# Cross attention's first scores inside the last query set, and masked attention's weight copies ahead of its scalings

## The reference, cut to what matters

```python
# masked ("sparse") attention: 8 heads of 64, one key/value head, blocks of 128 queries;
# each query sees its top keys by an index score
logits = q @ k_sel * 64 ** -0.5          # masked
p = softmax(logits); a_out = p @ v_sel
x = x + concat(a_out, b_out) @ w_out     # b_out: a 31-tap convolution, normed
# cross attention: 4 heads of 256, 256 memory rows
hq = rmsnorm(x); qc = hq @ w_q_cross
p = softmax(qc @ kc.T * 256 ** -0.5); oc = p @ vc
x = x + oc @ w_o_cross
```

## Time and profile before

| | us |
|---|---|
| median of 3 runs | 1608.12 (1607.89 to 1609.03) |
| the profiled execution | 1606.36 |
| its span | 1604.5 |
| PE busy | 1559.0 (97% of the span) |
| DVE busy | 1081.9 (67%) |
| ACT busy | 422.6 (26%) |

### The profile page before, as it was taken

One profiled execution on the slowest core, in us unless ns is written; L12 is line 12 of the kernel. 1 busy time (PEld: TensorE's weight loads), 2 busy tenths in 40 slices (PEclk: granted clock), 3 DMA queues, 4 the chain that ended last, 5 costly groups with the idle time before them and its releaser, 6 DMA issues.

```text
span 1604.5 us, 24121 instructions
## 1 busy us (share of the span) xinstructions
PE 1559.0 (97%) x9302; PEld 1110.9 (69%) x9302; DVE 1081.9 (67%) x2124; ACT 422.6 (26%) x823; POOL 136.2 (8%) x127
## 2 busy tenths in 40 slices
PE   7999999999999999999999999999999999999997
PEld 7885544456666666858544666478877888888886
DVE  5975857954545454668679896566768877876453
ACT  3345374421111010410255666201211100100001
POOL 0020020030000001000048400000000000000000
PEclk9999999999999999999999999999999999999999
DMA  7122111111111111242212222221022222223331
GB/s 269 66 79 79 53 53 53 53 40 43 49 59 41 45 40 52 94 147 80 79 53 67 93 67 91 72 79 60 27 92 82 90 79 89 96 79 98 87 92 66
DMA packets 48721, 121.63 MB, mean 76 GB/s; under 512 B 5408, under 2 KB 19488, under 8 KB 48352
## 3 DMA queue, kind: packets, MB, share of 16 engines
q1 hardware_dynamic: 47520, 116.41, 21.8%
q10 hardware_dynamic: 864, 2.37, 0.4%
q0 software_dynamic: 224, 1.31, 0.2%
HBM read 117.98 MB, written 2.10 MB: 75 GB/s over the span
## 4 chain that ended last, share of the span: by engine, by line
PE 56%; DVE 11%; issue 1%; ACT 1%; DVEq 0%; ACTq 0%
PE bank L618 5%; PE vpair L1359 4%; PE opair L1359 4%; PE apair L1359 3%; PE bank L1359 3%; PE bank L758 3%; PE vpair L648 3%; PE opair L648 3%; PE opair L1388 2%; PE vpair L1388 2%; DVE arena L1955 2%; PE apair L648 2%; DVE arena L2656 2%; PE apair L1388 2%; PE bank L1388 2%; PE bank L648 2%
## 5 line engine op out<-in xcount | busy, mean ns | idle before, releaser
L618 PE MATMUL bank<-h,ring 128*128 128x512 f32 x560 | 254.1, 596 | 0.8 <-ACTq L1508 0.8
L618 PEld LDWEIGHTS bank<-h,ring 128*128 128x128 f32 x560 | 102.8, 190 | 115.7 <-issue 111.4
L1946 DVE TENSOR_TENSOR arena<-ring 128x512 f32<-128x512 f32 (+2 forms) x148 | 90.2, 609 | 73.8 <-DMA ring<-weights 47.8
L618 PE MATMUL bank<-arena,ring 128*128 128x512 f32 (+1 forms) x320 | 121.1, 518 | 1.4 <-ACT arena L1512 1.4
L1955 DVE SCALAR_TENSOR_TENSOR arena<-arena,cols 128x512 f32<-128x512 f32 (+1 forms) x129 | 94.8, 735 | 4.6
L618 PEld LDWEIGHTS bank<-arena,ring 128*128 128x128 f32 x320 | 57.5, 190 | 41.9 <-issue 35.7
L1946 DVE TENSOR_TENSOR arena<-arena,vpair 128x256 f32<-128x256 f32 x47 | 19.8, 421 | 93.8 <-PE vpair L1084 50.1
L2932 POOL TENSOR_TENSOR arena<-arena 128x512 f32<-128x512 f32 x47 | 61.6, 1310 | 10.5 <-ACT arena L1805 6.9
L2937 POOL TENSOR_TENSOR h<-h,sq 128x512 f32<-128x512 f32 x2 | 2.5, 1266 | 697.8 <-ACT sq L1915 697.7
L1946 DVE TENSOR_TENSOR arena<-arena 128x256 f32<-128x256 f32 (+1 forms) x114 | 57.6, 505 | 6.0 <-PE bank L969 2.2
L758 PE MATMUL bank<-x,arena 128*128 128x256 f32 x192 | 54.9, 409 | 0.0
(11 more groups left out here) (392 smaller groups left out, 3239.4 us busy)
## 6 DMA issues: line engine op xcount, KB each, us to landing
ring<-weights SPq DMA_DIRECT2D x169, 512.0 KB, 3.6
ring<-weights SPq DMA_DIRECT2D x36, 256.0 KB, 3.6
ring<-weights SPq DMA_DIRECT2D x68, 128.0 KB, 2.3
x<-xt SPq DMA_DIRECT2D x8, 512.0 KB, 7.9
ring<-weights SPq DMA_DIRECT2D x40, 64.0 KB, 2.0
out<-h SPq DMA_DIRECT2D x8, 256.0 KB, 2.2
cst<-cst_in ACTq DMA_DIRECT2D x1, 1056.0 KB, 9.6
arena<-mem2t POOLq DMA_DIRECT2D x1, 1024.0 KB, 5.0
```

The costliest lines, as they stand in the source:

```text
L618: last = mm(o[:, 0:n], weight(), src, start=c == 0, stop=c == len(srcs) - 1)
L1946: do(V.tensor_tensor(out, a, b, op), sig)
```

## The change: what it does

1. Masked attention, ScalarE: in odd steps the copy of the transposed weights of job i-2, and the reading of projected groups that follows it, stands ahead of scaling(i-1) and exponential(i). Even steps are as before.
2. `fast_stage` becomes a generator, `fast_sets`, which can stop in a set behind its fourth product. Of the last query set PE issues four products, then scores(0) and scores(1) of cross attention, then in step 1 the other three products. In step 2, behind scores(2), it waits until VectorE has taken the last set, whose banks the transposes and outputs use. VectorE takes the last set behind step 1 and writes its queries behind step 2.
3. Cross attention's heads come in the order 0, 2, 1, 3, and the operand sums of "cross o" in the order of tiles 0, 4, 2, 6. PE waits for all eight query tiles in front of scores(4), and "cross o" for six instead of four outputs in front of its first product.

```diff
-            for hd in range(4):
+            for hd in (0, 2, 1, 3):
...
                     product(d[:, HT:T], lambda k: w[12 + k], lambda k: t_of[3][:, k])
                     if n == 0:
                         pe.wait_ge(dense_dve.sem, reads("dve", g - 1))
+                    if n in split:
+                        yield
...
-            fast_stage("cross q", h, h_tiles, h_tiles, {0: square_sum})
+            queries = fast_sets("cross q", h, h_tiles, h_tiles, {0: square_sum}, (FAST - 1,))
+            next(queries)
             pe.wait_ge(dense_dve.sem, reads("dve", start["cross o"] - 2))
             pe.wait_ge(qc_ready.sem, 4)
-            attention(cross_jobs(), inject={1: [lambda: pe.wait_ge(qc_ready.sem, 8)]})
-            fast_stage("cross o", oc, lambda: pe.wait_ge(o_read.sem, state["o"] - 4), lambda: pe.wait_ge(o_read.sem, state["o"]))
+
+            def rest_of_queries():
+
+                finish(queries)
+                yield
+                pe.wait_ge(dense_dve.sem, reads("dve", start["cross o"] - 1))
+                yield
+
+            attention(cross_jobs(), rest_of_queries(), lambda i: (int(i in (1, 2)), 0, 0),
+                      inject={3: [lambda: pe.wait_ge(qc_ready.sem, 8)]})
+            fast_stage("cross o", oc, lambda: pe.wait_ge(o_read.sem, state["o"] - 2), lambda: pe.wait_ge(o_read.sem, state["o"]))
...
+                    def weights_in():
+
+                        nk, _, score, *_ = jobs[i - 2]
+                        o = a_in()
+                        st["pt"] += 1
+                        if st["pt"] > 2:
+                            act.wait_ge(o_done.sem, st["pt"] - 2 + (i >= 4 and paired_with(i - 4, first)))
+                        w = len(score) * nk
+                        do(fn(bufs["att"][1][:, (st["pt"] - 1) % 2, 0:w], o[:, 0:w], ACT.Copy), pt_ready)
+                        a_read_inc()
+                        read_through(reading, stage_, issued(fills, i - 1) + fills(i)[0])
+
+                    ahead = outputs and i % 2 == 1
+                    if ahead and 2 <= i <= n + 1:
+                        weights_in()
                     if outputs and 1 <= i <= n:
...
-                    if 2 <= i <= n + 1:
...
+                    if not ahead and 2 <= i <= n + 1:
+                        weights_in()
...
-            for n in range(FAST):
-                fast_take("cross q", n)
+
+            def queries(n):
+
                 for c in range(2):
                     tt(qc[:, n + 4 * c, :], tmp[:, c], ri, MUL, qc_ready)
+
+            for n in range(FAST - 1):
+                fast_take("cross q", n)
+                queries(n)
                 if n + 2 < FAST:
                     fast_weights("cross q", n + 2)
-            signal_now(norm_applied)
             after = {i: (lambda i=i: fast_weights("cross o", i // 4, [i % 4])) for i in range(8)}
+            after[1] = lambda: (fast_take("cross q", FAST - 1), fast_weights("cross o", 0, [1]))
+            after[2] = lambda: (queries(FAST - 1), signal_now(norm_applied), fast_weights("cross o", 0, [2]))
             after[5] = lambda: (fast_weights("cross o", 1, [1]), fast_operand(oc, 0, 2))
-            after[7] = lambda: (fast_weights("cross o", 1, [3]), fast_operand(oc, 2, 2))
-            after[9] = lambda: fast_operand(oc, 4, 2)
+            after[7] = lambda: (fast_weights("cross o", 1, [3]), fast_operand(oc, 4, 2))
+            after[9] = lambda: fast_operand(oc, 2, 2)
             after[11] = lambda: fast_operand(oc, 6, 2)
```

More of the change, by code:

```diff
@@ L636, in dense_normed, with fast_sets @@
                 end_group(last)
-            def fast_stage(name, src, first_half, second_half, after_set={}):
+            def fast_sets(name, src, first_half, second_half, after_set={}, split=()):
                 for n in range(FAST):
@@ L676, in fast_stage @@
                         after_set[n]()
+            def fast_stage(*stage_of):
+                finish(fast_sets(*stage_of))
             def group_read(g):
```

## The result

| | before | after |
|---|---|---|
| median, us | 1608.07 (20 runs, 1606.38 to 1609.09) | 1611.01 (20 runs, 1609.20 to 1612.31) |
| the profiled execution | 1606.36 | 1609.62 |
| its span | 1604.5 | 1607.8 |

The ratio is 1.0017, with a 95% interval of 1.0011 to 1.0024: the change costs 2.9 us (1.8 to 3.9 by the interval). The forecast was +1.2 with a range up to 1611.9: the sign was right, the time lies in the range of 8 in 10, and more than half of the loss was not in the sum. The time is just over the forecast's own range (1608 to 1611). The prediction took 3.2 us for about what a measurement can tell; the loss is a little less, and its interval lies above a ratio of 1.

A forecast was written before the change was run, and what follows sets the result against it. PE is busy 97%, but VectorE and ScalarE set the time in masked attention up to 957.23, and VectorE just before cross attention's end. Masked +1.48, cross -0.28: +1.2 on 1608.12 gives 1609.3 us, 8-in-10 range 1604.3 to 1611.9.

The forecast's parts named there:

- VectorE 2.37 us late at reciprocal(3), through ScalarE's wait for job 1's transposes: Masked attention, step 3: ScalarE idles until PE's transposes are done, making VectorE 2.37 us late, never made up.
- Some 0.5 us more at step 7, never made up: Masked attention: a copy ahead of exponential(7) makes VectorE lose some 0.5 us more, 2.87 in all.
- The 2.27 us gap stays as a sum, part of it in front of score blocks: Masked attention, PE's wait for copy(5): the copy starts as before, so 2.27 us stays, part moving to score blocks.
- Step 16 +1.48, and it stays: Masked attention: behind copy(13), PE's value products start at 958.71 instead of 957.23, +1.48 us, and the shift stays.
- The taps' end is covered: VectorE's convolution taps after masked attention end at 989.9, before PE asks for them: 2.6 us or more of slack.
- Scores(2) without a gap, scores(3) with 0.65, scores(4) 1.79 early: Start of cross attention: PE's 1.72 us gap goes, 0.65 replaces 0.70, scores(4) start at 1114.25 against 1116.04.
- Three operand sums instead of one on the chain, a gap of about 2 us at transposes(7), output stage 0.28 early: End of cross attention: VectorE's operand sums add 1.46 us, taking back the head start except 0.28 us.
- rival 3: Masked attention: VectorE's delay reaches PE whole, +2.9; with cross attention's operand sum +4.4, 1612.5 us; chance 0.10.
- 1 (gaps go as named): Both stages: PE's gaps are won, masked attention -3.3, cross attention -1.8, together -5.1, 1603.0 us; chance 0.10.
- 2 (the cross part moves alone, 1606.1): ScalarE's step 3 wait costs VectorE under 1.4 us, only cross attention gains: about -2, 1606.1 us; chance 0.17.
- 4 (both terms under 0.5): Masked and cross attention: nothing comes of the change, both terms under 0.5 us, 1608.1 us; chance 0.08.

The follow-up runs named there:

- Experiment 4: Changed kernel plus two PE products that nobody reads, in the gap ahead of transposes(7): 1609.54 us, ratio to before 1.0007.
- experiment 2: Changed kernel with ScalarE's masked attention put back as before, so only the cross-attention part remains: 1609.13 us, ratio to before 1.0005.
- 3: Changed kernel with cross attention's operand sums all behind step 9, none behind step 7: 1608.10 us, ratio to before 1.0000.
- experiment 5: Kernel before with the masked-attention copy moved ahead in step 3 and in no other: 1610.44 us, ratio 1.0012.
- experiment 9: Changed kernel with copies ahead only from step 7 on, and the operand sums all behind step 9 of cross attention: 1605.20 us, ratio to before 0.9981.
- experiment 6: Kernel before with the masked-attention copy moved ahead only in odd steps from 9 on: 1608.04 us, ratio 0.9998.
- experiment 7: Changed kernel with copies ahead only from step 9 on, and the operand sums all behind step 9 of cross attention: 1605.94 us, ratio to before 0.9987.
- 8: Changed kernel with copies ahead from step 5 on, operand sums behind step 9, later convolution taps two in odd steps and one in even: 1606.54 us.
- 1: Kernel before with the masked-attention part of the change alone: 1609.72 us, ratio 1.0009.

## Why the prediction was right, and where not

- *VectorE 2.37 us late at reciprocal(3), through ScalarE's wait for job 1's transposes:* right to a hundredth (3.32 of wait for 3.3, and net 2.37 late). It is one block, not many small ones.
- *Some 0.5 us more at step 7, never made up:* right. Reciprocal(7) waits 0.58 us, and the taps end 2.9 late.
- *The 2.27 us gap stays as a sum, part of it in front of score blocks:* right (0.80 + 0.51 + 0.52 and a little besides). The prediction has no word of a gap at the fill in step 8, which is 2.09 us. PE comes there early, with a clock of 1.00 in 926 to 930 where before has 0.50 and 0.81; as PE is not what sets the time there, neither counted.
- *Step 16 +1.48, and it stays:* +1.51, and alone +1.53.
- *The taps' end is covered:* right, VectorE is idle for 7.89 us behind it.
- *Scores(2) without a gap, scores(3) with 0.65, scores(4) 1.79 early:* no gap, 0.70, and 1.45. Steps 2 and 3 on VectorE have small waits between dependent operations that I had not counted, some 0.2 us up to maximum(3); the other 0.15 lie between it and scores(4).
- *Three operand sums instead of one on the chain, a gap of about 2 us at transposes(7), output stage 0.28 early:* the place and the gap (1.97) are right. This is the step that failed: transposes(7) came net 0.08 late, which is 0.36 off, and **the sum went on as if PE kept its speed behind a gap of 2 us**. It didn't: the 16 products took 5.12 instead of 3.69 us at a granted clock of 0.50, +1.42. The gap was named in the prediction, the rows of before already held one like it with eight products in 1.98 us behind it, and I didn't ask why these took twice what others of their form take (1.08 us). The term of cross attention was therefore +1.50 in place of -0.28. Experiment 4 shows that the idle time is its cause, experiments 2 and 3 that the cross part alone makes it and that moving the sums removes it.
- *The size.* The measured +2.9 lies 1.7 from the forecast's +1.2 and 1.5 from rival 3's +4.4. That the time is in the range of 8 in 10 is owed to its width, which was meant for other errors; no term of the range was a fall of the clock.
- *The rivals.* 1 (gaps go as named) fell: the gap was broken up and not won. 3 (VectorE's delay reaches PE whole, by waits in further odd steps) fell: there are no such waits. That a delay can reach PE whole is seen in experiment 5, where copy(13) keeps its place: 2.37 of 2.37. 2 (the cross part moves alone, 1606.1) fell twice over: ScalarE's wait cost 2.37 and not under 1.4, and the cross part lost. 4 (both terms under 0.5) fell with +1.51 and +1.50.
- *"Optimization Strategy" of the Trainium skill's page "Perfetto Trace Analysis"*, by which what releases a gap of the most contended engine is made to start sooner: in after the trace disagrees (+1.5). In experiment 9, with the edit kept to the steps in which ScalarE has not to wait, the gap at the value products of step 8 goes (2.27 to none), a wait of 2.08 us turns up at the fill behind them, and the 0.85 gained at step 16 come from the later steps' copies (the gap at step 16 falls from 1.04 to 0.49).

**What stays open.** Why the clock falls behind some gaps of about 2 us and not behind others. Behind 2.27 us it fell in before and in experiment 6, and not in 7. Behind 2.12 us it fell in 5 (at 920.66), and behind 2.09 us in 8 (at 932.74), but not behind the 2.08 to 2.10 us of the same fill in after, 1 and 9. Length alone does not decide it.

The runs of after are of two kinds: 13 of 20 lie at 1610.9 to 1612.3 with a mean granted clock of 0.992 to 0.993, 7 at 1609.2 to 1609.6 with 0.994 to 0.995. Before has two kinds as well, 18 at 1607.8 to 1609.1 and 2 at 1606.4. Both profiled executions are of the shorter kind, so the account of 3.29 us is theirs; kind by kind the medians differ by 3.1 and 3.4 us. What the longer kind loses was not profiled in after or before. The profiles of the experiments make a guess: in eight of the ten the clock is at 0.96 instead of 1.00 both in 400 to 440 and in 480 to 520, in the recurrent branch, which the change does not touch (2 has the second fall alone, 3 a deeper one in 320 to 360 in place of the first), and in 1, for one, VectorE's work comes 1.3 us later behind each of the two. That makes the base offsets near 2 us. Whether such falls are more frequent in after than in before the runs do not tell.

## What to carry to other kernels

Before an instruction is moved ahead on an engine that works in order, ask what it waits for itself and who waits for what it overtakes: here one copy moved ahead in a step in which its operand was not ready cost 2.37 us, the same move from four steps later on cost VectorE 0.59 us and still let the stage gain 0.85. A head start is worth only what the last common wait lets through, so walk it to the end of the stage: two operations of 0.7 us in the wrong step took all of it. And price a gap of about 2 us on PE at more than its length, since what runs behind it may run at half the clock (16 products in 5.12 us instead of 3.69 here, and in other profiles nothing).

## What the hardware showed that was not expected

- Behind an idle time of PE of only 1.97 us (after) and 1.96 us (experiment 2), and 2.27 us (before, experiment 6), the granted clock was at 0.50 for a few us, and came back by itself; it cost 1.4 us in after. In before it lies in 926 to 928, behind the gap at 925.70, and VectorE, which sets the time there, has no wait behind it. In experiment 6 the same fall reached VectorE, by 1.21 us.
```profile
926.00:928.00 2.00, 2.00 (x10) 0.93 (x7) 1.86 (x6) 0.88 (x3) 0.00 (x0) 0.50 0.00 0
```
- Products of no use in that gap, 1.88 us of them, made the kernel 1.5 us faster by the medians (1611.01 to 1609.54; ratios to before 1.0017 (1.0011 to 1.0024) and 1.0007 (0.9998 to 1.0016)).
- The same gap of 2.27 us, at the same place and with the same work on both sides, left the clock at 1.00 in experiment 7, and step 16 came 1.18 us sooner than in 6.
